# A float32 kernel of three transformer layers: opening loads on GpSimd's queue, gating one block later, a mean from a running sum, and a layer norm spread over three blocks

## What is computed

```python
h = rmsnorm(x, g_pre)                      # g_pre: 2048 gains
proj = h @ w_in                            # qkv, z_a, b_raw, a_raw, glu_in, z_b, gate_logits
# branch a: short conv of qkv, silu, l2norm; beta, g_log from b_raw, a_raw (the "decays")
o_a = gated_delta_chunked(q, k, v, g_log, beta)        # 16 heads
o_a = rmsnorm(o_a, g_dn_out) * silu(z_a);  y_a = o_a @ w_br_a
# branch b: u = glu(glu_in), 31-tap depthwise conv over the tokens, plus b_dw
u = silu(layernorm(u, ln_g, ln_b)) * silu(z_b);        y_b = u @ w_br_b
gate_a, gate_b = split(sigmoid(gate_logits + b_gate))
x = x + rmsnorm((gate_a * y_a + gate_b * y_b) @ w_out, g_post)
```

## Time and profile before

| what | value |
|---|---|
| median of 3 runs | 2203.95 us (2203.84 to 2204.75) |
| profiled execution, its own time | 2203.62 us |
| its span, first to last instruction | 2201.8 us |
| mean granted TensorE clock | 0.992 of full speed |
| instructions | 29122 |
| bytes moved | 431.31 MB, 196 GB/s on average |

### The profile page before, as it was taken

How to read it: one execution, slowest core, us unless ns; L and a number is a source line. 1 busy time by engine, 2 the same in 40 slices (tenths; PEclk the granted TensorE clock), 3 DMA queues, 4 the chain that set the end, 5 groups by cost and what they waited for, 6 DMA issues and landing times.

```text
span 2201.8 us, 29122 instructions
## 1 busy us (share of the span) xinstructions
PE 2141.1 (97%) x10062; PEld 1770.1 (80%) x10062; DVE 1477.1 (67%) x2747; ACT 1237.5 (56%) x2388; POOL 308.5 (14%) x417
## 2 busy tenths in 40 slices
PE   6999999999999998999999999999999899999996
PEld 5788888888888887887788887888788688888885
DVE  4778777789999885566665564653566654456665
ACT  4666666677777763445555554554354355555542
POOL 0111111146565631010000000000000000000000
PEclk9999999999999999999999999999999999999998
DMA  5866766678877766674766565565545365554452
GB/s 177 251 194 189 212 200 194 198 208 238 245 208 216 219 216 199 200 256 156 245 228 221 191 213 192 175 207 161 194 164 199 130 199 188 189 169 137 163 199 95
DMA packets 431954, 431.31 MB, mean 196 GB/s; under 512 B 29472, under 2 KB 305072, under 8 KB 430304
## 3 DMA queue, kind: packets, MB, share of 16 engines
q1 hardware_dynamic: 416048, 381.69, 55.3%
q0 software_dynamic: 5920, 26.68, 3.6%
q10 hardware_dynamic: 9872, 21.50, 2.6%
HBM read 406.72 MB, written 23.09 MB: 195 GB/s over the span
## 4 chain that ended last, share of the span: by engine, by line
PE 91%; DVE 4%; ACT 1%; issue 1%; DMA 1%; SPq 1%; POOL 0%; DVEq 0%; ACTq 0%; POOLq 0%
PE pair L439 27%; PE pair L441 27%; PE pair L440 27%; DVE w_lo L419 1%; PE QA L1410 1%; PE RA L1426 1%; PE RA L586 1%; PE QB L1495 0%; PE QA L1061 0%; SPq L387 0%; DMA vec<-in_b_gate_dram 0%; PE RA L1651 0%; PE RB L1651 0%; ACT ub L1320 0%; PE RA L772 0%
## 5 line engine op out<-in xcount | busy, mean ns | idle before, releaser
L419 DVE TENSOR_TENSOR w_lo<-raw,w_hi 128x512 fp32r<-128x512 f32 x1376 | 926.3, 693 | 425.7 <-ACT w_hi L413 425.2
L413 ACT ACTIVATE w_hi<-raw 128x512 fp32r<-128x512 f32 x1376 | 833.4, 626 | 466.5 <-PE pair L441 455.8
L439 PE MATMUL pair<-w_hi,in_hi 128*128 128x512 f32 x2368 | 950.7, 401 | 8.9 <-DVE w_lo L419 4.7
L441 PE MATMUL pair<-w_hi,in_lo 128*128 128x512 f32 x2368 | 925.3, 391 | 0.0
L440 PE MATMUL pair<-w_lo,in_hi 128*128 128x512 f32 x2368 | 923.7, 390 | 0.0
L439 PEld LDWEIGHTS pair<-w_hi,in_hi 128*128 128x128 f32 x2368 | 446.1, 188 | 98.1 <-DVE in_lo L1080 5.1
L441 PEld LDWEIGHTS pair<-w_hi,in_lo 128*128 128x128 f32 x2368 | 445.5, 188 | 95.6
L440 PEld LDWEIGHTS pair<-w_lo,in_hi 128*128 128x128 f32 x2368 | 446.6, 189 | 88.5 <-issue 1.0
L983 POOL TENSOR_TENSOR acc_p<-acc_p,tap 128x256 f32<-128x256 f32 x160 | 181.7, 1135 | 38.9 <-ACT tap L967 25.4
L967 ACT ACTIVATE tap<-upad,cwl 128x256 f32<-128x256 f32 x192 | 96.6, 508 | 49.7 <-POOL acc_p L983 48.8
L1014 DVE SCALAR_TENSOR_TENSOR QB<-upad,cwl,QB 128x256 f32<-128x256 f32 x272 | 119.8, 480 | 0.0
(11 more groups left out here) (396 smaller groups left out, 1771.6 us busy)
## 6 DMA issues: line engine op xcount, KB each, us to landing
raw<-in_w_in_dram SPq DMA_DIRECT2D x512, 256.0 KB, 3.7
raw<-in_w_in_dram SPq DMA_DIRECT2D x80, 1024.0 KB, 5.1
raw<-in_w_out_dram SPq DMA_DIRECT2D x48, 1024.0 KB, 5.0
raw<-in_w_kv_shared_dram SPq DMA_DIRECT2D x24, 1024.0 KB, 5.0
raw<-in_w_br_a_dram SPq DMA_DIRECT2D x16, 1024.0 KB, 5.5
raw<-in_w_br_b_dram SPq DMA_DIRECT2D x16, 1024.0 KB, 5.8
raw<-in_w_mem_kv_dram SPq DMA_DIRECT2D x16, 1024.0 KB, 4.9
raw<-in_w_ple_gate_dram SPq DMA_DIRECT2D x16, 1024.0 KB, 4.9
```

Of the source, the lines that this page charges most:

```text
L413: act.activation(w_hi[:, u % 2, q % UK], raw[:, u, q % UK], ACT.Copy).then_inc(hi_ready[u], 1)
L419: dve.tensor_tensor(w_lo[:, u % 2, q % UK], raw[:, u, q % UK], w_hi[:, u % 2, q % UK].bitcast(F32), ALU.subtract)\
L439: pe.matmul(o, xh, wh, start=(q == 0), stop=False)
L441: mm = pe.matmul(o, xl, wh, start=False, stop=(q == KC - 1))
```

## The change

- ROW_TILES is cut so that g_pre has a tile of its own. SP issues the identity and g_pre, then block 0's weights at once. All other small loads are issued by POOL, first ba_raw, constants, dt_bias, a_log, g_dn_out, then the nine row loads.
- x is loaded in two halves of channels, each with its own semaphore. PE begins with g_pre's transpose and turns groups 0 to 3 once the first half is there. The other seven row tiles are transposed in block 0, at hs 20 to 26 (ROWS_AT is 19), after the decays.
- SP issues block 1's weights before the decays' store and the load of gc_b.
- The product of the rule's output with orn and z moves from hs 29 to hs 4 of the next block (`og_dve`); PE's, ACT's and DVE's steps behind it move from hs 7, 9, 9 to 8, 10, 11, the load of the next z from hs 6 to 9.
- vec is loaded by POOL early in the B blocks.
- POOL adds each group's u into `usum` (one add of 128 x 256 per group), and the mean takes one product `ones` by usum, at hs 14 of block 36.
- The norm: centring at hs 2, 6, 24, 28 of block 37, the reciprocal at hs 3 of block 38, the quarters from hs 6, 18, 30 of block 38 and hs 10 of block 39 on, the last ub_lo at hs 22 of block 39. The reloads of ub and zb are waited for by halves.

```diff
-ROW_TILES = [(CH_GPRE, 64), (CH_SHORT, 96), (CH_SHORT + 96, 96)] + [(CH_LONG + 124 * i, 124) for i in range(4)]
+ROW_TILES = [(CH_GPRE, 16), (CH_LNG, 48), (CH_SHORT, 96), (CH_SHORT + 96, 96)] + [(CH_LONG + 124 * i, 124) for i in range(4)]
...
     def oa_pe(pe, g, hs):
-        if hs == 7:
+        if hs == 8:
...
-        if hs == 29:
+    def og_dve(dve, g, hs):
+        if hs == 4:
             dve.wait_ge(s["pool_b"], 2 * g + 2)
...
+    def add_u_pool(pool, j, par):
+        pool.wait_ge(s["u_ready"], j + 1)
+        if isinstance(j, int) and j == 0:
+            pool.tensor_copy(usum[:, :], ubz[:, par, 1]).then_inc(s["u_added"], 1)
+        else:
+            pool.wait_ge(s["u_added"], j)
+            pool.tensor_tensor(usum[:, :], usum[:, :], ubz[:, par, 1], ALU.add).then_inc(s["u_added"], 1)
...
-        reach(pool, s["u_ready"], j)
+        if not isinstance(j, int) or j > 0:
+            add_u_pool(pool, j - 1, 1 - par)
...
     def start_sp(sp):
-        sp.dma_start(const[:, K_ID:K_ID + P], t["shape_constants"][:, K_ID:K_ID + P]).then_inc(s["rows_in"], 16)
-        vecs = [t[n].rearrange("a (r c) -> (a r) c", c=P) for n in ("g_pre", "ln_g", "ln_b", "b_dw")]
...
+        sp.dma_start(const[:, K_ID:K_ID + P], t["shape_constants"][:, K_ID:K_ID + P]).then_inc(s["gain_in"], 16)
+        sp.dma_start(rows[0:KC, 0], t["g_pre"].rearrange("a (r c) -> (a r) c", c=P)).then_inc(s["gain_in"], 16)
+
+    def small_loads_pool(pool):
+        pool.dma_start(ba_raw[:, :, :], w_in[:, :, COL_BA:COL_BA + 2 * HEADS]).then_inc(s["ba_in"], 16)
+        pool.dma_start(const[:, P:], t["shape_constants"][:, P:]).then_inc(s["ba_in"], 16)
...
+    def rows_loads_pool(pool):
+        vecs = [t[n].rearrange("a (r c) -> (a r) c", c=P) for n in ("ln_g", "ln_b", "b_dw")]
         for i, v in enumerate(vecs):
+            pool.dma_start(rows[16 * i:16 * (i + 1), 1], v).then_inc(s["rows_in"], 16)
...
     def start_pe(pe):
-        pe.wait_ge(s["rows_in"], 16 * (4 + len(ROW_TILES)))
+        pe.wait_ge(s["gain_in"], 32)
+        pe.transpose(QA[:, 0:KC], rows[0:KC, 0], ident[0:KC, 0:KC]).then_inc(s["rows_cols"], 1)
+            if g % 4 == 0:
+                pe.wait_ge(s[f"x_in{g // 4}"], 16)
+    def rows_pe(pe, hs):
+        i = hs - ROWS_AT
+        if 0 < i < len(ROW_TILES):
+            at, n = ROW_TILES[i]
+            if i == 1:
+                pe.wait_ge(s["rows_in"], 16 * (len(ROW_TILES) + 1))
+                pe.wait_ge(s["gc_copied"], 3)
...
     def start_act(act):
+        for c in range(2):
+            half = slice(c * D // 2, (c + 1) * D // 2)
+            act.dma_start(x_tok[:, :, half], tokens(t["x"][0])[:, :, half]).then_inc(s[f"x_in{c}"], 16)
...
-    LN0 = 32 * (BLK_Y + 2 - BLK_GB)
+    LN0 = 32 * (BLK_Y - BLK_GB)
+    MEAN_AT, CENTRE_AT, RSTD_AT, SCALE_AT = 14, (34, 38, 56, 60), 67, (70, 82, 94, 106)
...
-            for j in range(4 * c, 4 * c + 4):
-                mm = pe.matmul(QA[:, 0:S], ones, ub[:, j], start=(j == 0), stop=(j == KC - 1))
+        if at == MEAN_AT:
+            pe.wait_ge(s["u_added"], KC)
+            pe.wait_ge(s["oa_lo_done"], 2 * NG)
+            pe.matmul(QA[:, 0:S], ones, usum[:, :], start=True, stop=True).then_inc(s["var_done"], 1)
...
     def _(sp):
         start_sp(sp)
         load_heads(sp, 0, COL_A, 0)
+        load_heads(sp, 1, COL_A, 1)
         decays_sp(sp)
-        load_heads(sp, 1, COL_A, 1)
```

More of the change, by code:

```diff
@@ L171, in program @@
     x_squares = sb("x_squares", [P, D])
+    rows = sb("rows", [P, len(ROW_TILES), P])
+    assert spot[0] <= at_b
     spot[0] = at_b
-    rows = sb("rows", [P, len(ROW_TILES), P])
     ba_raw = sb("ba_raw", [P, KC, 2 * HEADS])
@@ L1050, in rule_buffers_pool @@
         pool.wait_ge(s["pads_ready"], 10)
+        pool.dma_start(vec[:, :], t["b_gate"][0, D:2 * D].partition_broadcast(P)).then_inc(s["vec_loaded"], 16)
     BANKS = (QA, QB, RA, RB)
@@ L1150, in start_act @@
     def start_act(act):
-        for tile in range(TT):
-            act.dma_start(x_tok[:, tile], tokens(t["x"][0])[:, tile]).then_inc(s["x_in"], 16)
-        act.wait_ge(s["chan_ready"], len(ROW_TILES))
+        for c in range(2):
+            half = slice(c * D // 2, (c + 1) * D // 2)
+            act.dma_start(x_tok[:, :, half], tokens(t["x"][0])[:, :, half]).then_inc(s[f"x_in{c}"], 16)
+        act.wait_ge(s["chan_ready"], 1)
         turn_act(act, 0, in_hi, scale=chan[:, CH_GPRE:CH_GPRE + KC])
@@ L1191, in start_dve, with rows_dve @@
     def start_dve(dve):
-        for i, (at, n) in enumerate(ROW_TILES):
+        dve.wait_ge(s["rows_cols"], 1)
+        dve.tensor_copy(chan[:, 0:KC], QA[:, 0:KC]).then_inc(s["chan_ready"], 1)
+        turn_dve(dve, 0, in_hi, in_lo, scale=chan[:, CH_GPRE:CH_GPRE + KC])
+    ROWS_AT = 19
+    def rows_dve(dve, hs):
+        i = hs - ROWS_AT
+        if 0 < i < len(ROW_TILES):
+            at, n = ROW_TILES[i]
             dve.wait_ge(s["rows_cols"], i + 1)
             dve.tensor_copy(chan[:, at:at + n], (QA, QB)[i % 2][:, 0:n]).then_inc(s["chan_ready"], 1)
-        turn_dve(dve, 0, in_hi, in_lo, scale=chan[:, CH_GPRE:CH_GPRE + KC])
     def decays_first_dve(dve):
@@ L1322, in norm_b_act @@
             ins.then_inc(s["ln_affine"], 1)
-        if at >= 24 and (at - 24) % 8 == 0 and at < 24 + 32:
-            c = (at - 24) // 8
+        if at - 4 in SCALE_AT:
+            c = SCALE_AT.index(at - 4)
             act.wait_ge(s["ln_affine"], c + 1)
@@ L1327, in norm_b_act @@
             act.activation(sqb[:, c % 2], ub[:, 4 * c:4 * c + 4], ACT.Tanh, scale=0.5).then_inc(s["ln_tanh"], 1)
-        if at >= 30 and (at - 30) % 8 == 0 and at < 30 + 32:
-            c = (at - 30) // 8
+        if at - 10 in SCALE_AT:
+            c = SCALE_AT.index(at - 10)
             act.wait_ge(s["ln_gated"], c + 1)
@@ L1347, in norm_b_dve @@
                .then_inc(s["ln_scaled"], 1)
-        if at >= 26 and (at - 26) % 8 == 0 and at < 26 + 32:
-            c = (at - 26) // 8
+        if at - 6 in SCALE_AT:
+            c = SCALE_AT.index(at - 6)
             x = ub[:, 4 * c:4 * c + 4]
@@ L1776, in beside_act @@
             rule_act(act, blk - BLK_GB, hs)
-        if BLK_GB < blk < BLK_Y and hs == 6:
+        if BLK_GB < blk < BLK_Y and hs == 9:
             act.wait_ge(s["og_ready"], blk - BLK_GB)
@@ L2002, in reload @@
             pool.dma_start(to[:, half], ubz_dram[half, :, i].rearrange("k p n -> p k n")).then_inc(s["ubz_loaded"], 16)
-        load(vec[:, :], row_of(t["b_gate"][0, D:2 * D]), "vec_loaded")
         for g in range(NG):
             rule_pool(pool, g)
+            if g == 0:
+                add_u_pool(pool, KC - 1, (KC - 1) % 2)
         pool.wait_ge(*step("o_done1", NG - 1))
@@ L2015, in tail_pool @@
         gate_a(2)
+        after(ubz_loaded=16)
         reload(ub, 1, 1)
+        after(ubz_loaded=32)
+        reload(zb, 0, 0)
         pool.wait_ge(psum_free, BLK_Y + 2)
         gate_a(3)
-        after(ubz_loaded=32)
-        for c in range(2):
-            reload(zb, 0, c)
+        after(ubz_loaded=48)
+        reload(zb, 0, 1)
         after(ub_hi_done=4, ln_gated=4)
@@ L2133, in _, with decays_beside @@
         tail_sp(sp)
-    def decays_beside(first, then, eng, turn=None):
+    def decays_beside(first, then, eng, turn=None, rows=None):
         def between(hs):
+            if rows:
+                rows(eng, hs)
             if hs == 2:
@@ L2218, in _ @@
             lo_piece(dve, 0, q)
-        dve_block(dve, 0, decays_beside(decays_first_dve, decays_dve, dve))
+        dve_block(dve, 0, decays_beside(decays_first_dve, decays_dve, dve, rows=rows_dve))
         dve.wait_ge(s["gc_stored"], 32)
```

84 lines of the change are left out of this document (41 added, 43 removed).

## The result

| kernel | median of 4 runs | lowest to highest | ratio to before, 95% |
|---|---|---|---|
| before | 2203.89 us | 2203.51 to 2204.75 | |
| after | 2185.69 us | 2184.19 to 2186.98 | 0.9919 [0.9907, 0.9932] |

The change makes the kernel 18.2 us faster. The forecast was 2175.7 us, 28.2 us less than before, with a range to 2185.5 us: the direction was right, the gain 10 us smaller, and the time lies 0.2 us beyond the range (two of its four executions lie inside it).

What follows compares the result with a forecast made beforehand. TensorE, busy 97% of the span, was taken as the bound, so only its work and waits count. Terms summed to -28.2 us from 2203.62, giving 2175.4 us, median 2175.7 us; range 2171.5 to 2185.5 us.

Steps and rivals of the forecast that it cites:

- Block 1's weights ahead of gc_b: Block 1: earlier weight loads remove TensorE's waits of 1.06 and 1.44 us, -2.5 us; the later gc_b stays hidden.
- Opening, weights: Before block 0's first product: weight unit 0 lands at 14.3 us, about when ScalarE wants it, +0.3 us.
- rival 1: Opening bound by bytes at one shared rate, unit 0 only at 17.6 us, total 2180.2 us; chance 0.10.
- x first: Opening: TensorE starts turning x at some 6.2 us instead of 15.11, second half of x hidden; -8.9 us.
- Clock: Opening: the half-speed stretch after the first product keeps its loss of some 3.0 us, so 0 change.
- Rival 4: Opening's half-clock stretch falls into the turning of x, 3.0 us more gain, total 2172.7 us; chance 0.05.
- Rule, block 33: Block 33: TensorE's wait for x goes, -5.9 us, and half of the half-clock loss behind it, -2.8 us.
- rival 2: TensorE's rule wait moves to hs 7, for tt behind og, three times; +5.7 us, total 2180.4 us; chance 0.10.
- Norm spread: Norm blocks: spreading VectorE's norm work over 48 half-steps removes TensorE's waits of 2.6 and 1.8 us, -4.4 us.
- Rival 3: The norm still lags because VectorE is nearly at capacity; the 4.4 us stay, total 2180.1 us; chance 0.06.
- GpSimd's sum: Conv blocks: sixteen adds of u fit into GpSimd's idle time, 0 us; without that cover +13 us.
- Rival 5: GpSimd's loads run one after another, row tiles reach block 0 131 us late, total 2306 us; chance 0.03.

Runs made afterwards that it cites:

- the third experiment: The changed kernel with GpSimd waiting for the second half of x before issuing its small loads; 2181.91 us.
- the kernel with three mends: The changed kernel with block 1's weights split around gc_b's store and load, GpSimd's loads behind x, and each add of u behind the group's first tap add; 2175.46 us.
- the short sum: The changed kernel with GpSimd's add of u into usum covering only 8 of 256 columns; 2182.21 us.
- the weights in halves: The changed kernel with SP issuing block 1's units 0 and 1, then the decays' store and load, then units 2 and 3; 2177.98 us.

## Why the prediction was right and where it failed

The step that failed is *Block 1's weights ahead of gc_b*, in its last word: "Hidden, with 4 us of cover." It was to bring -2.5 us. The 1.1 of them ahead of block 1 came, but block 1 got 5.7 us longer in place of 1.4 shorter: 7.1 us of the miss of 9.3. Two things were wrong in it.

- The landing. I had about 55 us, and it was 60.4: the store went out at 47.8 and not at 45.9 us, 3.8 us passed to the next issue and not 1.6, and the load took 8.8 and not 7.2 us.
- What is wanted first. I counted DVE's wait against chunk 6 of the weights. PE wanted `conv` first, at 67.9 us, and 11.8 us of DVE's chain stood between the landing and it. So gc_b was due at 56.1 us, and the cover, even with my landing, was 1.1 us and not 4. By the prediction's own start of block 1, 50.8 us where it was 52.88, there was none.

Of the other terms:

- *Opening*: -6.3 us for -8.6. The second step that failed is *Opening, weights*, the tie taken at +0.3 us. Unit 0 was there at 17.7 us and not at 14.3, which is rival 1's 17.6: from 1.9 to 17.7 us 4.6 MB were moved, at 290 GB/s, where 3.95 MB at 0.32 MB per us had been counted. In *x first* two readings failed. g_pre, taken to be there, held the turn until 7.09 us, and the late bound for the second half, 8.9 us, was no bound: it landed at 12.5 us. With the small loads later (first product at 17.26 us in the third experiment, -8.2 us) the opening is nearly as forecast.
- *Block 0*: -0.1 us for +0.1, by errors that cancel. *Decays*: `ba_lo` was waited for, 1.4 us, with 1.6 us of cover forecast. *Row transposes*: POOL's loads were in time, and the seven cost 1.1 us for 1.2. *Clock*: the stretch at half clock is there still, but only from 19.7 to 23.1 us, 3.4 in place of 6.9 us, which gives back some 1.7 us. With the wait of 1.1 us at 59.30 us that is gone, the sum is 1.1 + 1.4 - 1.7 - 1.1 = -0.3 us.
- Rival 4 came in at most in part. In the turn the transposes start 0.21 us apart throughout, where the later half of them was 0.11 us apart within a group before, and the half-clock stretch behind is shorter. The granted clock stands at 1.00 during the turn, so it doesn't show this pace.
- *Rule, block 33*, with *new behind og*: -7.3 us for -7.7. PE waits 0.6 us for `tt`, once, so rival 2 is out in its size. Blocks 34 and 35 cost 0.8 us, for 0. The list of waits has one that is new there, for `vn`, once in each of blocks 33 to 35 and 0.2 us long. It is there too with the gating back at hs 29, so it doesn't come from the gating's place; its cause was not tested.
- *Mean*: 6.44 us for 6.5.
- *Norm spread*: blocks 37 to 40 give -14.3 us. Less 6.9 us of the mean's products that is 7.4 us, all but 0.2 of it in block 39 (28.93 to 21.76 us), for 4.1 us net. The lag was read from the list of waits, 2.6 + 1.8 us, and the products that run up to a wait were not counted. Rival 3 is out.
- *GpSimd's sum*: +1.8 us for 0. The cover named was GpSimd's idle time, and the price was paid by DVE: the step that failed is that an add in POOL's idle time costs nothing.
- Rival 5, the loads in series, is out: POOL issued one after the other.

The errors by stretch sum to +2.3 - 0.2 + 7.1 + 1.8 + 0.4 + 0.9 - 3.3 + 0.3 = +9.3 us, the 28.2 us less the 18.9 of the spans. The forecast of 2175.7 us is about the time of the kernel with three mends, but not by its own terms: 3.3 us of the norm stand in it against 1.8 us of the adds and other small losses.

What stays open: why executions of one kernel lie apart, those of after by 2.8 us and those of before by 1.2 us in the first comparison and by 2.4 to 3.7 us beside the experiments. One part can be seen at the opening. The half-clock stretch there differs between kernels that are the same up to there: from 19.7 us for 3.4 us in after, from 19.1 us for 3.4 us with the quarters every 8, from 13.1 us for 10.2 us with the gating at hs 29, where it does reach into the turning of x, and from 17.6 us for 10.3 us with the short sum, where block 0 takes 1.8 us longer. With the weights in halves and with GpSimd's loads after x the granted clock is 1.00 all through the opening, and yet the first products of block 0 start 0.43 us apart; so the column doesn't tell the whole pace. What starts and ends such a stretch was not tried.

## What to carry to other kernels

An engine that waits in its program order holds back everything behind it, so the time at which a transfer is due is that of the first thing wanted of the whole chain behind, less the length of that chain, and a small load queued behind bulk loads is late by all of them. Two waits that lie over each other have to go together: each alone brought 0.1 and 1.7 us, both 7.3. Measure a lag by the length of the block against an undisturbed one, not by the listed waits, and ask of work given to an idle engine whom it slows down beside it.

## What the runs showed of the chip

- Small loads on GpSimd's queue held up large ones issued just before and beside them. In the eight kernels that issue them beside x, x's second half landed 9.5 to 11.4 us after its issue, and ACT got the first unit of weights at 17.5 to 18.4 us, after a wait. In the two kernels that issue them behind x it landed after 7.7 and 7.8 us, and ACT began that unit at 15.6 and 15.0 us without a wait.
- An add of 128 x 256 on GpSimd, 0.75 us long, stretched the DVE operation beside it from 0.42 to between 0.82 and 0.95 us, and another from 0.68 to 1.08 us. It cost TensorE 1.8 us over six blocks in after, and between 1.5 and 2.9 us in the other kernels with the full add; why it differs is not shown.
- A lagging stretch costs TensorE more than its idle time: 3.6 us of waits went with 5.75 us of length, and 4.34 us of waiting for `conv` with 4 us of products at nearly half their pace behind it.
